# When VectorE makes the third quad sums of the FFN openings, and when GpSimd starts the sums of the following body

## The reference

```python
def conv_ffn(x, w_in, conv_w, conv_b, w_out):
    h = causal_dwconv(x @ w_in, conv_w, conv_b)
    gate, val = h[..., :D_FF], h[..., D_FF:]
    return (jax.nn.gelu(gate) * val) @ w_out
```

## Time and profile before

| | us |
|---|---|
| median of 3 runs | 3266.76 |
| lowest and highest | 3265.27 and 3268.62 |
| the profiled execution, device time | 3266.88 |
| its span in the trace | 3265.2 |
| TensorE busy | 3180.4 |
| mean granted TensorE clock | 0.995 |

### The profile page before, as it was taken

How to read it: one execution, slowest core, us unless ns; L and a number is a source line. 1 busy time by engine, 2 the same in 40 slices (tenths; PEclk the granted TensorE clock), 3 DMA queues, 4 the chain that set the end, 5 groups by cost and what they waited for, 6 DMA issues and landing times.

```text
span 3265.2 us, 49903 instructions
## 1 busy us (share of the span) xinstructions
PE 3180.4 (97%) x16674; PEld 2557.2 (78%) x16674; DVE 1912.3 (59%) x3860; ACT 1075.8 (33%) x2383; POOL 1551.0 (48%) x1383
## 2 busy tenths in 40 slices
PE   8999999999999999999999999999999999999998
PEld 7787888867777788886446888868888688788887
DVE  6676667455555566746437555466763534476754
ACT  3533333123333233313326343123331334223322
POOL 4343887323221388742001444448863431468843
PEclk9999999999999999999999999999999999999999
DMA  3223223211111222221210111222222211222231
GB/s 133 83 84 123 78 84 104 78 58 59 59 53 39 97 78 102 89 93 46 67 50 28 64 58 58 78 78 101 88 103 72 69 55 66 78 78 84 98 104 52
DMA packets 68767, 250.60 MB, mean 77 GB/s; under 512 B 7568, under 2 KB 7568, under 8 KB 68544
## 3 DMA queue, kind: packets, MB, share of 16 engines
q1 hardware_dynamic: 68544, 247.72, 22.0%
HBM read 245.59 MB, written 2.10 MB: 76 GB/s over the span
## 4 chain that ended last, share of the span: by engine, by line
PE 88%; DVE 7%; ACT 2%; issue 2%; DMA 0%; DVEq 0%; POOL 0%; SPq 0%; ACTq 0%; POOLq 0%
PE psum L2670 27%; PE psum L2716 25%; PE psum L779 6%; PE psum L2607 5%; PE psum L2901 4%; PE psum L2198 3%; PE psum L1731 3%; PE psum L1758 2%; PE psum L2223 1%; PE psum L811 1%; PE psum L2913 1%; PE psum L1785 1%; DVE scratch L3462 1%; PE psum L849 1%; ACT scratch L1445 1%
## 5 line engine op out<-in xcount | busy, mean ns | idle before, releaser
L3773 POOL TENSOR_TENSOR scratch<-scratch 128x512 f32<-128x512 f32 (+1 forms) x440 | 475.3, 1090 | 143.4 <-PE psum L2716 74.5
L2670 PE MATMUL psum<-scratch 128*128 128x256 f32 (+2 forms) x2080 | 506.1, 381 | 1.4 <-DVE scratch L3511 1.3
L2670 PEld LDWEIGHTS psum<-scratch 128*128 128x128 f32 x2080 | 394.4, 190 | 61.6 <-DVE scratch L3511 3.7
L3511 DVE TENSOR_TENSOR scratch<-scratch,psum 128x256 f32<-128x256 f32 (+2 forms) x720 | 299.2, 422 | 204.3 <-PE psum L2670 184.4
L2716 PE MATMUL psum<-scratch 128*128 128x256 f32 (+2 forms) x1856 | 414.3, 381 | 0.2
L2716 PEld LDWEIGHTS psum<-scratch 128*128 128x128 f32 x1856 | 352.2, 190 | 52.3 <-issue 1.6
L3479 DVE SCALAR_TENSOR_TENSOR psum<-scratch,params,psum 128x256 f32<-128x256 f32 (+2 forms) x704 | 312.7, 485 | 55.8 <-ACT psum L3087 55.8
L3711 POOL TENSOR_TENSOR scratch<-w_ring 128x512 f32<-128x512 f32 (+2 forms) x56 | 69.7, 1245 | 409.3 <-PE psum L2716 204.7
L2989 ACT ACTIVATE scratch<-psum 128x256 f32<-128x256 f32 (+2 forms) x216 | 82.5, 385 | 550.8 <-PE psum L2716 527.8
L3107 ACT ACTIVATE scratch<-psum 128x256 f32<-128x256 f32 (+2 forms) x320 | 123.2, 385 | 408.9 <-PE psum L2670 404.6
L2716 PE MATMUL psum<-acts,scratch 128*128 128x256 f32 (+2 forms) x976 | 223.1, 384 | 4.9 <-DVE stream L3343 3.7
(11 more groups left out here) (541 smaller groups left out, 6057.9 us busy)
## 6 DMA issues: line engine op xcount, KB each, us to landing
w_ring<-units SPq DMA_DIRECT2D x335, 512.0 KB, 3.5
scratch<-units SPq DMA_DIRECT2D x128, 512.0 KB, 4.2
residual<-x_t SPq DMA_DIRECT2D x4, 528.0 KB, 7.2
out_t<-residual SPq DMA_DIRECT2D x2, 512.0 KB, 3.4
out_t<-residual SPq DMA_DIRECT2D x1, 768.0 KB, 4.4
params<-cols SPq DMA_DIRECT2D x1, 568.5 KB, 11.4
out_t<-residual SPq DMA_DIRECT2D x1, 256.0 KB, 3.3
gate_w_sb<-gate_w SPq DMA_DIRECT2D x1, 96.0 KB, 10.5
```

What stands on the lines that cost most here:

```text
L2670: mm = nc.tensor.matmul(PS[:, bank, 0:H], weights(q), moving(q), start=(opens and q == 0), stop=(q == 1), skip_group_check=True)
L3511: v.tensor_tensor(row, row, PS[:, rank_bank(j, at), 0:H], ALU.add if sign > 0 else ALU.subtract).then_inc(r_later, 1)
L3773: g.tensor_tensor(blocks([RANK_BUFFERS + o for o, _, _ in sums]), blocks([a for _, a, _ in sums]), blocks([e for _, _, e in sums]), ALU.ad ...
```

## The change

A new constant `MOVED_FIRST = 14` sets two things.

- VectorE, in all four FFNs, makes the moving sums 2 to 13 and then the quad sum "22" of q = 0, then moving sum 14, then the quad sum "22" of q = 1, then moving sum 15. Before, both quad sums came behind moving sum 15. Nothing is added or removed.
- GpSimd gets one wait ahead of its first sum for the first rank body: until moving sum 13 is made.

```diff
+MOVED_FIRST = 14
...
                 quad_sum("11", 2, 1, 0)
                 quad_sum("11", 2, 1, 1)
-                for q in range(2, last_kept):
+                for q in range(2, MOVED_FIRST):
                     rank_moving(q)
                 quad_sum("22", 5, 3, 0)
+                rank_moving(MOVED_FIRST)
                 quad_sum("22", 5, 3, 1)
+                for q in range(MOVED_FIRST + 1, last_kept):
+                    rank_moving(q)
                 quad_sum("12", 3, 2, 0)
                 quad_sum("12", 3, 2, 1)
...
                 if j == 1:
                     pool.wait_ge(q_weight, weight_ready(0, b, 4, 1))
+                    pool.wait_ge(r_moving, rank_moved(n, MOVED_FIRST - 1))
```

## The result

The changed kernel takes 3245.12 us (median of 4 runs, 3243.14 to 3247.07) against 3266.45 us of the kernel before in the same set, a ratio of 0.9934 with a 95% interval of 0.9917 to 0.9951. That is 21.3 us less; the forecast was 3243.6 us. The profiled execution took 3243.14 us, 23.7 us less than the profiled one of before. Two later sets, the second of them on another chip than the first, gave the changed kernel 3249.14 and 3248.93 us, with the ratios 0.9945 (0.9932 to 0.9959) and 0.9953 (0.9937 to 0.9968).

What follows compares the result with a forecast made beforehand. TensorE, busy 97%, was taken as the bound, losing 24.8 us in four FFN openings to waits for VectorE's quad sums and slow matmuls behind them. 15.68 + 9.10 - 1.6 = 23.2 us off gave 3243.6 us, range 3240.0 to 3251.0.

Steps and rivals of the forecast that it cites:

- The wait ahead of product 3: TensorE's idle time in four FFN openings, waiting for VectorE's quad sum "22" of q = 0; 15.68 us, all gone.
- By this part alone a wait of 1.4 us would stay: Moving the quad sums on VectorE, without holding GpSimd, still leaves TensorE waiting 1.4 us before product 3.
- Moving sum 13 ends 3.3 us earlier: With GpSimd held back, VectorE's sums 2, 4, 12, 13 are unstretched; sum 13 ends at 316.7, not 319.96.
- The clock behind it: Product 3 ran slowly at a lowered clock after TensorE's wait in four FFNs; the excess, 9.10 us, all gained.
- GpSimd's backlog: First rank body: GpSimd, starting later, lags 1.6 us more; TensorE stalls 0.4 us per FFN, 1.6 us in all.
- best end: No stall in the first rank bodies and TensorE's 1.3 us wait for line 3511 gone too; 3240.7 us.
- evenly shared alternative: VectorE and GpSimd share the SBUF port evenly: GpSimd's six sums take 9.1 us, against turn-taking's 1.2 us hold-up.
- The sum: Whole program: 15.68 + 9.10 - 1.6 = 23.2 us off, giving 3243.6 us.
- Rival (a): First rank bodies: GpSimd's backlog becomes the new bound, 18.4 us off, 3248.4 and up to 3251; chance 0.14.
- Rival (b): VectorE's stretched sums aren't due to GpSimd; TensorE still waits 1.4 us each, 3249.2 or 3258.3; chance 0.04.
- rival (c): Openings: product 3 waits for something that comes no earlier, so nothing is gained; 3266.8 us; chance 0.03.
- Rival (d): First rank body starves behind GpSimd and the kernel gets slower; 3278.4 us at a lag of 8 us; chance 0.04.

Runs made afterwards that it cites:

- GpSimd later: Changed kernel with GpSimd's first sum for the first rank body held until the second quad sum "22" is made; 3253.85 us, ratio 0.9958.
- wait only: Kernel before plus only GpSimd's wait until moving sum 13 is made, VectorE's order as before; 3245.99 us, ratio 0.9933.
- order only: Changed kernel without the wait on GpSimd, so only VectorE's quad sums "22" moved; 3246.09 us, ratio 0.9938.

## Why the prediction was right

- **The wait ahead of product 3** (15.68 us): gone in all four FFNs. The two steps that led to it were each shown apart. "By this part alone a wait of 1.4 us would stay": 1.3 us measured with the order alone. "Moving sum 13 ends 3.3 us earlier": it ends at 315.11 + 1.32 = 316.43, 1.08 us after product 5 starts at 315.35; before it was 319.96 - 315.61 = 4.35 us after, so 3.3 us.
- **The clock behind it** (9.10 us): the mechanism is right, the size holds for one execution. Product 3 takes 3.56 us and the clock is 1.00. With the start times the openings gain 25.43 us, 0.65 more than 15.68 + 9.10, since the profile's idle time is counted from a modelled end. But in the second profile of the kernel before the openings lose only 23.2 us. The 9.10 us should have been a range of 7 to 9, and the forecast stood at its better end.
- **GpSimd's backlog** (1.6 us of stall): the mechanism is right; the stall was larger than forecast and its net cost smaller. GpSimd's last sum ends at 338.84, 16.37 us behind the start of the rank body, before 345.10 - 329.95 = 15.15: a lag of 1.2 us where I had 1.6. The first bodies are 0.6 to 1.2 us longer in all, but that is a net figure. The timeline's rows of ffn0 are:

```profile
331.41 1.13 PE L2671 MATMUL psum<-norm_mu,scratch 128*128 128x264 f32 x4
...
334.34 1.16 PE L2671 MATMUL psum<-scratch 128*128 128x264 f32 x4
...
338.90 1.16 PE L2671 MATMUL psum<-residual,scratch 128*128 128x264 f32 x4
```

  Each product of that body should follow the one before by 0.89 us. The one at 331.41, the eleventh, comes 0.93 us behind its neighbour at 330.48 and takes 0.08 us longer than the others; the one at 338.90, the nineteenth, starts right behind GpSimd's last sum and takes 0.11 us longer. With start times taken this way in all four FFNs of the first profile, what is lost at the products that need GpSimd's newest sums is 0.2 us in ffn0 and 0.6 in each of the others, 2.1 us in all, and more of it lies ahead of the tenth and eleventh products than at the nineteenth. In exchange the fourteenth product (334.34 here), which waited for VectorE's line 3511 before, loses 1.2 us in the four FFNs where it lost 2.5. The forecast had this gain only in its best end. So the stall was a third larger than 1.6 us, and 1.2 us of it was given back.

  The Trainium skill ("SBUF — State Buffer", on the two sides) has VectorE's and GpSimd's instructions take the shared port pair by turns, the second blocked until the first has ended. The trace agrees with it: beside moving sums 14 and 15, which keep to 0.73 and 0.70 us, GpSimd's second and third sums take 1.64 and 1.80 us in place of 1.29, 0.9 us more where 1.2 had been counted.

```profile
316.56 1.29 POOL L3778 TENSOR_TENSOR scratch<-scratch 128x512 f32<-128x512 f32 x1 [14.54 <-DVE scratch L3463]
317.93 3.40 POOL L3778 TENSOR_TENSOR scratch<-scratch 128x512 f32<-128x512 f32 x2
```

  The evenly shared alternative would have made the lag 2.8 us, and it was 1.2.
- **The sum**: 24.6 us from start times in the FFNs, against 23.2 forecast. The medians show 21.3, 17.4 and 15.1 us. The step missing in the working is that of the rest of the program, which I took as fixed: its length differs by up to 7 us between executions of the changed kernel, and over all runs 4 to 6 us of the gain come back there as a lower clock. That the first median came within 1.5 us of the forecast is therefore in part luck; the other two are 5.5 and 5.3 us above it. The range, 3240.0 to 3251.0, held all three medians, but it was made for GpSimd's backlog, which was not what moved them.
- **Rival (a)** would have needed the lag of 2.8 us; "GpSimd later" shows that the price of such a lag was rated somewhat high, 0.8 us for a us and not one. **Rival (b)** fell with "wait only", **rival (c)**, that nothing is gained, with the openings of the changed kernel. **Rival (d)** is the same slope as "GpSimd later", from a lag that didn't arise.

## What to carry to other kernels

A wait of TensorE costs its length and then the slow matmuls behind it, so look at the duration of the same product before and behind the wait before rating it; here 15.7 us of idle time stood for 23 to 25 us. When one engine's work is late, ask both what is queued ahead of it and what runs beside it on the engine that it shares a port with: either answer removed most of the loss here, and the two gains didn't add. If the instruction can be moved far enough ahead, that is better than holding the other engine back: here by 1 to 2 us in the FFNs, and each us of further holding cost 0.8 us once the slack was gone. A gain read in one stage need not arrive in the whole: of 22 to 25 us in the FFNs the mean of all runs shows 18.

## What the runs showed of the hardware

- Behind waits of TensorE of 1.0 to 1.2 us (the four openings of "order only") the clock stayed at 1.00; behind 2.2 to 2.3 us it was down in one of four; behind 3.8 to 4.0 us in all eight seen, and the slow matmuls then took 1.6 to 3.1 us more, differently in each execution of the same program.
- VectorE's moving sums with both inputs in SBUF took 0.70 us alone and up to 1.8 us beside GpSimd's sums, and GpSimd's sums of 128 x 512 took 1.3 us alone and up to 1.87 beside them; the quad sums with one input in PSUM took 0.41 to 0.43 us in either case.
- Two sets of runs of one kernel can differ by 4 us in the median (3245.1 and 3249.1) with the same start times in all the places that were changed. Two profiled executions, compared stage by stage, showed where the difference lay; the medians alone did not.
